# Gate vectors turned into rows on TensorE before they are sent to DRAM, in a two-block transformer kernel

## What is computed

```python
mod = c_act @ w_ada[l] + b_ada[l]
sh_m, sc_m, gt_m, sh_f, sc_f, gt_f = jnp.split(mod[:, None, :], N_MOD, axis=-1)
...
x = x + gt_m * rms_norm(y, g_post_mix[l])
...
def _ffn_half(s, mod, g, wg, wu, wd):
    shift, scale, gate = mod
    h = _modulate(_rmsnorm(s, g), shift, scale)
    return s + 0.5 * gate * _swiglu(h, wg, wu, wd)
```

## Time and profile before

| what | us |
|---|---|
| median of 3 runs | 2540.37 |
| lowest and highest of them | 2532.43 and 2541.52 |
| the profiled execution | 2538.89 |
| its span in the trace | 2537.1 |

### The profile page before, as it was taken

The page is one execution under the profiler, slowest core; times in us unless marked ns, Lnnn a source line. Parts: engine busy times, 40 slices in busy tenths (PEclk is TensorE's granted clock), DMA queues, the critical chain, the costliest instruction groups (busy, mean ns, idle before and its releaser), DMA issues.

```text
span 2537.1 us, 34673 instructions
## 1 busy us (share of the span) xinstructions
PE 2413.1 (95%) x13098; PEld 2030.5 (80%) x13098; DVE 1678.4 (66%) x2618; ACT 1080.8 (43%) x1850; POOL 394.2 (16%) x431
## 2 busy tenths in 40 slices
PE   3899999989999999999979999999999999998998
PEld 3678987779989888887648888888888888777997
DVE  6957986857995776777965565565565565346454
ACT  4466545566554212236744322224322224345443
POOL 0111101111111101105850110110100100001101
PEclk9999999999999999999989999999999999999999
DMA  8655985546773554443212363443453444322662
GB/s 312 243 172 188 303 314 204 203 139 223 263 271 119 200 187 175 182 159 92 67 33 84 134 198 117 166 166 108 126 198 125 153 173 121 109 77 74 192 199 92
DMA packets 135879, 422.55 MB, mean 167 GB/s; under 512 B 28448, under 2 KB 32672, under 8 KB 135712
## 3 DMA queue, kind: packets, MB, share of 16 engines
q1 hardware_dynamic: 135152, 418.55, 48.4%
q10 hardware_dynamic: 560, 1.79, 0.2%
HBM read 419.17 MB, written 1.11 MB: 166 GB/s over the span
## 4 chain that ended last, share of the span: by engine, by line
PE 63%; DVE 3%; ACT 2%; POOL 1%; issue 1%; POOLq 0%; DVEq 0%; ACTq 0%
PE ps L1148 20%; PE ps L1150 20%; PE ps L1149 20%; PE ps L1343 2%; PE ps L1331 1%; POOL ap L2215 1%; ACT F L1465 1%; DVE sl L1694 1%; PE ps L1311 1%; PE ps L1366 0%; PE ps L1300 0%; DVE F L1812 0%; DVE ps L2040 0%; PE ps L1248 0%; ACT junk L1429 0%
## 5 line engine op out<-in xcount | busy, mean ns | idle before, releaser
L1406 ACT ACTIVATE sh<-raw 128x1024 fp32r<-128x1024 f32 x534 | 551.5, 1043 | 911.1 <-PE ps L1150 883.6
L1148 PE MATMUL ps<-hH,sh 128*128 128x256 f32 (+1 forms) x2560 | 842.6, 329 | 6.2 <-DVE hL L1783 3.5
L1149 PE MATMUL ps<-hL,sh 128*128 128x256 f32 (+1 forms) x2560 | 837.5, 327 | 0.0
L1150 PE MATMUL ps<-hH,sl 128*128 128x256 f32 (+1 forms) x2560 | 837.5, 327 | 0.0
L1694 DVE TENSOR_TENSOR sl<-raw,sh 128x1024 fp32r<-128x1024 f32 x534 | 640.2, 1218 | 100.7 <-ACT sh L1406 100.1
L1148 PEld LDWEIGHTS ps<-hH,sh 128*128 128x128 f32 x2560 | 484.8, 189 | 58.6 <-issue 7.3
L1149 PEld LDWEIGHTS ps<-hL,sh 128*128 128x128 f32 x2560 | 481.5, 188 | 49.1 <-issue 1.7
L1150 PEld LDWEIGHTS ps<-hH,sl 128*128 128x128 f32 x2560 | 481.2, 188 | 48.0
L1708 DVE CUSTOM_DVE_ANT_0 mjunk<-raw,cB,V 128x1024 bf16<-128x1024 f32 x384 | 499.4, 1301 | 28.2 <-DMA C<-in_cst 8.5
L2188 POOL TENSOR_TENSOR uLl<-F,uHh 128x256 fp32r<-128x256 f32 (+1 forms) x132 | 168.2, 1274 | 1176.7 <-ACT uHh L1583 1069.2
L1150 PE MATMUL ps<-sh,uLl 128*128 128x512 f32 x792 | 312.4, 394 | 0.0
(11 more groups left out here) (164 smaller groups left out, 2018.3 us busy)
## 6 DMA issues: line engine op xcount, KB each, us to landing
raw<-in_w SPq DMA_DIRECT2D x752, 512.0 KB, 4.7
G<-gates SPq DMA_DIRECT2D x14, 512.0 KB, 6.9
raw<-in_w SPq DMA_DIRECT2D x16, 256.0 KB, 4.3
cB<-in_rpb SPq DMA_DIRECT2D x64, 64.0 KB, 2.5
raw<-in_w SPq DMA_DIRECT2D x4, 492.0 KB, 6.4
S<-in_rows SPq DMA_DIRECT2D x6, 256.0 KB, 3.3
X<-in_x ACTq DMA_DIRECT2D x1, 1024.0 KB, 12.0
X<-in_ctx SPq DMA_DIRECT2D x1, 1024.0 KB, 7.9
```

The source lines that it names most:

```text
L1148: self.e.matmul(out, lh, rh, start=start, stop=False)
L1149: self.e.matmul(out, lh, rl, start=False, stop=False)
L1150: return self.e.matmul(out, ll, rh, start=False, stop=stop)
L1406: self.e.activation(self.m["sh"][k % SPL][:, 0:w], self.m["raw"][r % RAW][:, 0:w], ACT.Copy).then_inc(self.sems["w_hi"], 1)
```

## The change

The column tile is transposed by PE into a PSUM bank as 8 rows of 128 (`gturn`), ACT copies the rows to a new SBUF tile `gr` of 8 partitions (one for each stream), and SP sends these 8 rows of 512 bytes instead of 1024 numbers one by one. Between column and turn stands an idle side step, and the send is a side step of its own, so each gate now takes five side steps instead of three. The column tile is free when PE has read it, and the copy waits for the stream's previous send.

```diff
--- before.py
+++ after.py
@@ -183,7 +183,13 @@
         def fetch():
             self.add("gfetch", src=src, dst=dst, id=(gid, s), before=self.row_of.get(dst))
             self.row_of[dst] = (gid, s)
-        return ([lambda: self.add("gsend", src=src)] if src else []) + [fetch]
+        idle = lambda: None
+
+        def turn():
+            b = self.bank()
+            self.add("gturn", src=src, b=b)
+            self.left(b)
+        return ([idle, turn, lambda: self.add("gsend", src=src)] if src else []) + [fetch]
 
     def gates_later(self, name, l, v, g, streams, now=False):
         gid = self.new()
@@ -1061,12 +1067,11 @@
 
         src = s["src"]
         k = src[1]
-        dst = bass.AP(tensor=self.dram["gates"].tensor, offset=k * D, ap=[[1, P], [P, 8], [1, 1]])
-        self.wait_ge(self.got("gcol", src))
+        dst = bass.AP(tensor=self.dram["gates"].tensor, offset=k * D, ap=[[P, 8], [1, P]])
+        self.wait_ge(self.got("grow", src))
         self.wait_ge(self.own(f"G{k}"))
-        self.e.dma_start(dst, cut(self.m["gc"][:, k * 8:k * 8 + 1], [[1, 8], [1, 1]]),
-                         allow_slow_non_contiguous=True).then_inc(self.sems[f"gs{k}"], 16)
-        self.landed(f"gs{k}", ("sent", src), ("left", src))
+        self.e.dma_start(dst, self.m["gr"][k][:, :]).then_inc(self.sems[f"gs{k}"], 16)
+        self.landed(f"gs{k}", ("sent", src))
 
     def gfetch(self, s):
 
@@ -1137,7 +1142,7 @@
         self.parts = dict(start=self.start, proj=self.proj, prod=self.prod, down=self.down, turn=self.turn,
                           qturn=self.qturn, idx=self.idx, att_q=self.att_q, att_t=self.att_t, att_o=self.att_o,
                           taps=self.taps, ln_mean=self.ln_mean,
-                          ln_sq=self.ln_sq, u_free=self.u_free, join=self.join, warm=self.warm)
+                          ln_sq=self.ln_sq, u_free=self.u_free, join=self.join, warm=self.warm, gturn=self.gturn)
 
     def start(self, s):
         self.wait_ge(self.got("ones"))
@@ -1278,6 +1283,14 @@
                               start=True, stop=True)
         x.then_inc(self.sems["mm"], 1)
         self.done("mm", ("full", s["b"]))
+
+    def gturn(self, s):
+        src = s["src"]
+        self.wait_ge(self.gone(s["b"]))
+        self.wait_ge(self.got("gcol", src))
+        col = self.m["gc"][:, src[1] * 8:src[1] * 8 + 8]
+        self.e.transpose(self.buf(s["b"])[0:8, 0:P], col, self.m["C"][:, C_ID:C_ID + 128]).then_inc(self.sems["tr"], 1)
+        self.done("tr", ("full", s["b"]), ("left", src))
 
     def att_q(self, s):
         it, st = s["it"], s["st"]
@@ -1379,7 +1392,7 @@
                           glu1_a=self.glu1_a, glu1_b=self.glu1_b, glu1_c=self.glu1_c,
                           glu2_a=self.glu2_a, glu2_b=self.glu2_b, cglu_a=self.cglu_a, tap_w=self.tap_w, tap_p=self.tap_p,
                           ln_sq=self.ln_sq, ln_rstd=self.ln_rstd, ln_out=self.ln_out, v2=self.v2,
-                          u_free=self.u_free)
+                          u_free=self.u_free, gturn=self.gturn)
 
     def start(self, s):
         m, dram = self.m, self.dram
@@ -1482,6 +1495,14 @@
         self.wait_ge(self.got("h_f", p["id"]))
         self.e.activation(self.m["hH"][:, p["k0"]:p["k0"] + 4, c], F3, ACT.Copy).then_inc(self.sems["a_sb"], 1)
         self.done("a_sb", ("h_hi", p["id"]))
+
+    def gturn(self, s):
+        src = s["src"]
+        self.wait_ge(self.got("full", s["b"]))
+        if src[2]:
+            self.wait_ge(self.got("sent", (src[0], src[1], src[2] - 1)))
+        self.e.copy(self.m["gr"][src[1]][:, :], self.buf(s["b"])[0:8, 0:P]).then_inc(self.sems["a_ps"], 1)
+        self.done("a_ps", ("left", s["b"]), ("grow", src))
 
     def pout(self, s):
         cb, wd, mid = s["cb"], s["wd"], s["mid"]
@@ -2289,6 +2310,7 @@
                 m["mc"][(n, l)] = m["V"][:, at:at + wd]
         m["A"] = sb("A", [P, 32])
         m["gc"] = sb("gc", [P, 16])
+        m["gr"] = [sb(f"gr{i}", [8, P]) for i in range(2)]
         m["st"] = sb("st", [P, 32])
         m["den"] = sb("den", [P, 64])
         m["mst"] = sb("mst", [P, 16])
```

## The result

| what | before | after |
|---|---|---|
| median, us | 2534.84 (6 runs, 2532.2 to 2541.52) | 2557.77 (6 runs, 2556.31 to 2561.14) |
| the profiled execution, us | 2538.89 | 2558.56 |
| its span, us | 2537.1 | 2556.8 |

After to before is 1.008, with a 95% interval of 1.0067 to 1.0093. One of the 27 executions took 3015 us, and one of the 11 of run 4 took 6171; no ratio has them.

A forecast was written before the change was run, and what follows sets the result against it. PE was taken to bound the kernel, busy for 2413.1 of 2537.1 us. Terms of 2.7 + 3.1 + 7.1 + 0.8 + 3.4 = 17.1 us on 2538.9 gave 2556.0, stated as 2557; own range 2551 to 2562, wider range 2545 to 2565.

The forecast's parts named there:

- Turns on PE: Fourteen lone transposes on PE, at 0.10 + 0.08 us, say 0.19 each: 2.7 us, bounds 1.4 and 3.9.
- Flush stalls: In three half feed-forwards with four tiles, flushed turns wait for DVE's gate column, 1.03 us each: 3.1 us.
- The bank of the turn of O: Each mixer's tail: O's last transpose gets a bank gate1 still reads, 4.2 and 2.9 us later: 7.1 us, bounds 0 and 7.1.
- the clock: Lower granted clock behind PE's waits in both mixers' tails, 1.8 and 1.6 us: 3.4 us, bounds 0 and 6.2.
- all other shifts of banks: Later bank takers each move on by one; nearly all harmless, except two shifts, once in each mixer.
- The attention's transposes: In both mixers' attention, four transposes fall behind the wait for the output normalisation's bank: 0.8 us in all.
- The old sends: SP's 91.7 us of waits for 4-byte sends, hidden by split weights lying ready ahead of PE: removing them gains 0.
- Rival 1: Mixers' tail has slack, so bank and clock terms fall away: 2545.5 us, within 0.5%; chance 0.18.
- rival 2: Freed DMA queue brings loads sooner, ACT's 27.3 us of weight waits vanish: 2528.7 us, 0.4% faster; chance 0.05.
- Rival 3: Clock falls for longer, turns wait for columns or banks in more places: 2562.4 us or more; chance 0.14.
- Rival 4: Eight 512-byte pieces land no sooner than 12 us; time the same as the forecast; no separate chance given.

The follow-up runs named there:

- run 4: The kernel before, unchanged, measured and profiled a second time: 2536.83 us, ratio 0.9998 to the kernel before.
- Run 1: The kernel after, but the turn takes the third free bank ahead without moving the rotation on: 2540.58 us, ratio 1.0016 to the kernel before.
- run 6: The kernel before with the change's idle steps and the bank rotation moved on by one at each turn's place, no turn or copy: 2561.85 us.
- run 5: The kernel after, with turns, copies and banks kept, but the column sent again in 1024 pieces of 4 bytes after the copy: 2565.27 us.
- run 9: The kernel after with the longest-free bank rule, without the two early idle steps, and with 4-byte sends again: 2531.15 us, ratio 0.998 to the kernel before.
- run 3: The kernel after with turns not moving the bank rotation and without two early idle steps in four-tile feed-forwards: 2537.4 us, ratio 1.0002 to the kernel before.
- run 10: The kernel after with the longest-free bank rule, no early idle steps, and each gate's transpose done twice: 2518.27 us, ratio 0.9937 to the kernel before.

## Why the prediction held, and where its sum was off

The forecast of 2557 met 2557.77, and its cause is the one that the runs show. But the terms are less right than their sum, and that they met to 0.8 us is luck: the loss was 3 to 6 us larger than the 17.1 predicted, and the 2538.9 that it was added to lay 4 us above the 2534.84 that the kernel before had in six runs.

- **Turns on PE, 2.7 us.** Mis-sized (and 14 x (0.10 + 0.08) is 2.5, not 2.7). An isolated turn adds some 0.1 us (0.9 for the nine), so 14 make 1.4, the lower bound. The spacing alone was the price; the 0.08 for each change of kind did not come on top. The 0.275 us that the Trainium skill gives for a transpose of 128x128 in a kernel ("TensorE: Matmul & The Clock Gate", PE-mode transpose) is near this instruction's duration here (0.27), but most of it lies beside the neighbours.
- **Flush stalls, 3.1 us.** The place, the cause and the wait (1.01 of 1.03 us) were right. Each cost 1.59 us with its turn, because PE also loses some 0.5 us in stopping and starting again: this turn starts 1.41 us behind the matmul ahead of it, an isolated one 0.23, and the next matmul starts 0.34 behind the turn, in the other case 0.03.
- **The bank of the turn of O, 7.1 us, and the clock, 3.4 us.** The waits came as named, 4.75 and 3.42 us for some 4.7 and 3.4. Up to the gate multiply of the next tile the two tails lost 6.6 and 4.5 us, where 4.2 + 1.8 and 2.9 + 1.6 were expected: in the first mixer it comes 7.06 us later than before (212.54 against 205.48), of which the attention had brought 0.5. The clock was a little dearer than thought in the first: from the turn to the twelfth matmul behind it 5.6 us in place of 3.0, 2.6 more and not 1.8. What was missed stands behind that. I called all other shifts of banks harmless. The turns of the normed tile and the filler behind them now get banks that the gate multiplies still read (2.60 and 1.39 us in both mixers, in place of 0.89 and 1.77), and the granted clock falls again under the filler (0.80). In the first mixer the filler starts 9.05 us later and takes 7.72 us in place of 6.21, in the second 9.28 (row of 584.68), and so it becomes what the feed-forward waits for: 1.6 and 3.2 us more. Together the tails took 15.9 us, not 10.5. Run 1, where these waits are as before, and run 6, where they come back without any turn (2.59 and 1.39 us in the first mixer), show that they hang on the banks.
- **The attention's transposes, 0.8 us.** 1.02 us of wait in place of 0.57, twice; what was left of it behind the attention was 0.7.
- **The old sends, nothing.** (13 x 9.5 us of landing time are 124, not 120, which changes nothing.) Right to within 1.5 us for the kernel before: the weights lay ready behind nearly every send. The stretches of the earlier trace rows did not show the one wait for weights, 1.48 us at 760 us, and the reason as given was too general. It is true for where those sends stood; in the change's own places the same pieces cost 7 to 8 us at one late send (runs 5, 6 and 9), of which the wait itself is 4.9 to 5.4 and the lower clock behind it most of the rest. The advice of at least 512 bytes a transfer in the Trainium skill ("DMA: Bandwidth & Descriptors", Specifications) pays only in that case here.
- **What made the sum right.** The measured terms, 1.4 for the turns, 4.5, 0.7 and 15.9, make 22.5; the last two rows of the ledger brought this pair of profiles to 19.8. That the change caused either of them is not shown; the first, the wait at 760 us, is shorter in the mean with 512-byte pieces (run 4), the second differs as much between two executions of one kernel. The 17.1 predicted was 3 us too small against the one and 5 against the other: the turns were taken too dear, the flushes and the mixers' tails too cheap.

Rival 1 (slack in the tail) fell with runs 1 and 6, rival 2 (the queue pays) with run 3. Rival 3 (dearer) was right that more turns wait for banks and the clock stays low for longer, but in the mixers' tails, not behind the passes over weights. Rival 4 did not come: where SP waits for a send, the fetch follows it by about 4 us.

## What to carry to other kernels

A helper that takes one buffer from a rotation moves every later taker on, and the price lies where a taker meets a slow reader, far from the edit: follow each taker to whoever empties its buffer, all of them, and ask again behind each new wait. Giving out the buffer that was given back the longest ago, rather than the next in turn, removed most of this here, though single waits grew; it was worth 12 us to a kernel that nobody had thought at fault. A slow transfer is free only as long as what is queued behind it has stock ahead, so price it at its new place, not at its old one.

## What was not expected of the hardware

Back-to-back matmuls of 128x256 have two rhythms, 0.1133 and 0.1178 us apart, with PE at full clock and never idle. Which one a long stretch gets differs between executions of one program; the short ones of 192 matmuls in the second block ran at 0.1178 in all twelve profiles, and the last one of 528 at 0.1133. A rhythm holds for a whole feed-forward, over 1056 matmuls, unless a lone short instruction stands in between. In seven kernels with one turn in each of the first block's two feed-forwards the rhythm changed at the turn in 12 of 14 cases; in five profiles with none or with two it changed in 0 of 10. Both exceptions stayed at 0.1178. A third place, 529 matmuls with a turn at some 2400 us, says the same: 6 of 7 with one turn, 0 of 5 with none or two, and the exception stayed at 0.1178. Matmuls of 128x512 have more than one pattern as well, in one and the same profile of before: 0.231 and 0.236 us in turn from 810 to 870 us, and 0.226, 0.229 and 0.232 in turn from 350 to 400. The two rhythms would explain much of the spread of the kernel before, from 2532 to 2542 us: two feed-forwards at 4.7 us each. It may also be why the kernel after, with both rhythms in each of them, spreads over 4.8 us only (runs 1 and 3, which have a turn there as well, over 5.7 and 5.3 in 11 executions each, but run 9 over 7.1). Neither was tested by itself. That the count decides, odd against even, rests on run 10 alone; what in PE holds the rhythm, and how a program could choose the fast one, stays open. The Trainium skill ("TensorE: Matmul & The Clock Gate", Back-to-back issue gap) gives N / 2.4 + 2.5 ns for the isolated gap, which makes 109 ns for 256 columns. The rows here show two gaps at this width, both above it.
